# A ring of seven instead of eight buffers for expert rows, and four more rows of the output projection's weights kept on the chip

## The chip, the cores and the metric

One NeuronCore of a Trainium2 chip runs the whole step. Five engines work side by side: PE (matrix products), DVE (vector work), ACT (activations and scaled copies), POOL (here mostly the issuing of gathers) and SP (here only the issuing of transfers). The core's 16 DMA engines move data between HBM and the on-chip memory (SBUF). The metric is the device time in microseconds of one execution of the program; lower is better.

## What is computed

One layer of a hybrid decoder for 512 prompt tokens (behind 16 learned tokens) and 64 sample tokens. All data are float32. Cut to what matters here:

```python
xn = rmsnorm(hp, norm1[l])
qa, ka, va, qkv_b, z, b_raw, a_raw = project(xn, w_in[l], q_norm[l], k_norm[l])
...
hp = hp + merge_heads(oa, ob, z, lam_init, attn_subln[l], gdn_norm[l], w_out[l], hp.dtype)
hp = hp + peer_ffn(rmsnorm(hp, norm2[l]), peer_wq[l], peer_keys[l], peer_u[l], peer_v[l])
```

`merge_heads` ends in `y @ w_out`, the output projection (a 1024 x 1024 matrix). `peer_ffn` is the expert layer: every token picks 128 of 16384 experts (8 heads, 16 each); an expert is a row `u` and a row `v` of 1024 numbers:

```python
h = jnp.einsum('td,thkd->thk', xb, u[e]).astype(jnp.float32)
w = (gate * jax.nn.gelu(h, approximate=False)).astype(xb.dtype)
return jnp.einsum('thk,thkd->td', w, v[e])
```

## The kernel before

**Tokens.** They are worked on in four blocks of 128 prompt tokens and a last one with the 64 sample tokens (two experts of a sample token share a slot). A first phase, to some 480 us, projects all tokens, does the short convolution, the paged attention of the sample tokens and the first part of the delta network. In a second phase the experts of block t are worked off, and the attention, the output projection and the choice of experts of block t + 1 are done between them.

**A slot.** The second phase has 576 slots (128 for each prompt block, 64 for the last). For slot m POOL gathers one expert for each of 128 tokens: 128 rows of 2048 numbers (`u` and `v` side by side), 1 MB, into buffer m % RING of the tile `uv` (line 971). DVE multiplies `u` with the tokens and sums (line 1786), ACT makes the slot's weight (lines 1348, 1352) and puts it on a diagonal (line 1359), and PE adds weight times `v` to the block's sum by two products with that diagonal (line 2217). For 111 of the slots DVE adds `v` itself (line 1759). Only then is the buffer free. POOL issues gather m once the buffer of slot m - RING is free; it waits for that in front of every gather:

```python
if m >= RING and added_here(m - RING):
    pool.wait_ge(s_va, added_before(m - RING) + 1)
elif m >= RING:
    pool.wait_ge(s_vd, m - RING + 1 - added_before(m - RING))
```

**Order.** Every engine's order is fixed when the program is written: each piece of work is a generator that yields a due time, and `advance` emits the piece with the earliest one. In the second phase due times count slots; POOL emits what is due by `m - RING + USED` ahead of gather m, the other engines what is due by m.

**The output projection.** Its weights come in two halves of 512 output columns; a half has eight rows (128 x 512 numbers, 256 KB each). A block's products run in `mix` (line 2126; for the sample tokens line 2145) and take row k of a half by `mixer_row` (line 547). Rows 0 to 5 of the first half and rows 0 and 1 of the second stay in the tile `mix_kept` from the first block on (`KEPT = (6, 2)`, loaded by line 777). The other rows, two of the first half and six of the second, are loaded again for each block into `zone` (line 778), in which the expert layer's route weights follow (line 780, four loads of 2.25 MB a block). SP issues all of these, in `route_loads`.

**Room.** The last part of SBUF is used twice. In the first phase it holds the tokens turned round, the input weights, and other tiles, of which `taps`, the weights of the short convolution, lies near the end; in the second phase `uv` lies there.

Of the kernel before, what the change touches and what calls it, by code (L numbers as in the profile page):

```python
# [8 lines left out]
F32 = mybir.dt.float32  # L9
# [7 lines left out]
D = 1024  # L17
# [10 lines left out]
HW = NH * HD  # L28
CONV_W = 4
# [3 lines left out]
NT = PT + 1  # L33
# [38 lines left out]
PIECES = 6  # L72
PAGE_BUFFERS = 8
NPAIR = DB // 2
RING = 8
DIAGS = 4
WEIGH, SUM, USED = 0.4, 1.3, 1.5
NORMED = (9.2, 9.4)
# [2 lines left out]
ZONE = KC * HW + 4 * NK  # L81
FRONT = 11680
NEVER = 1.0e9
KEPT = (6, 2)
DMA_RING = 2048


# [88 lines left out]
def advance(streams, until):  # L176

    while min(s.due for s in streams) <= until:
        s = min(streams, key=lambda s: s.due)
        s.due = next(s.steps, NEVER)  # L180
# [55 lines left out]
def route_at(n, k):  # L236
    return SLOTS * (n - 1) + (74 + 1.05 * k if n < PT else 36 + 1.05 * k + (14 if k >= 4.9 else 0))
# [8 lines left out]
def hybrid_step(nc: bass.Bass, i, o, stay_table, early_table, past_table):  # L246

    ctx = ExitStack()
    with ctx:
        def keep(name, shape, dt=F32):  # L250
            return ctx.enter_context(nc.sbuf_tensor("sb_" + name, shape, dt))

        def stage(names):

            out = {}
            with ExitStack() as s:
                for name, (shape, dt) in names.items():
                    out[name] = s.enter_context(nc.sbuf_tensor("sb_" + name, shape, dt))
            return out

        def sem(name):
            return nc.alloc_semaphore(name)

        stay = keep("stay", [128, NSTAY])
        mix_kept = keep("mix_kept", [128, sum(KEPT), HW])
        minus_half = keep("minus_half", [128, 16])
        sizes = (HW, 2 * HW, 3 * HW, HW, NH * TOK, NT * HW, HW, NH * NSAMP, NH * 128)
        held = keep("held", [128, sum(sizes)])
# [21 lines left out]
        def st(name, rows=128, width=None):  # L290
# [19 lines left out]
        G = stage({  # L310
            "xn2": ([128, 2, D], F32), "q2T": ([128, 2, 4, 128], F32), "gain2T": ([128, KC], F32),
            "score": ([128, 4, 4, NK], F32),
            "Sw": ([128, 4 * NPOS + 2 * SEQ], F32), "wTm": ([META, 2, 128], F32),
            "nm": ([128, 2, 2], F32), "Z": ([128, 2, 2], F32), "rz": ([128, 2, 2], F32),
            "ass": ([128, NH], F32), "ams": ([128, NH], F32), "ars": ([128, NH], F32),
            "ss2": ([128, NT], F32), "ms2": ([128, NT], F32), "rstd2": ([128, NT], F32),
            "eidx": ([128, 2, SLOTS], U32), "best": ([128, 2 * TOPK], F32), "gate": ([128, 2, SLOTS], F32),
            "gmax": ([128, 2, TOPK], F32), "gsum": ([128, 2], F32),
# [6 lines left out]
        F.update(stage({  # L325
            "xnT": ([128, KC * TOK], F32), "w": ([128, PIECES, KC // 4, HW], F32), "wba": ([128, KC, 2 * NH], F32), "raw": ([128, 2, HW], F32), "qkn": ([128, 2, HW], F32),
            "qst": ([128, 2, HW], F32), "gains": ([128, 2 * DQ + HD], F32),
            "taps": ([128, CONV_W, HW], F32), "rstd": ([128, NT], F32), "ss8": ([128, 2, 8], F32), "ms8": ([128, 2, 8], F32), "rstd8": ([128, 2, 8], F32),
        }))
        G.update(stage({"uv": ([128, RING, 2 * D], F32)}))  # L330
        G["S"] = G["Sw"][:, 0:4 * NPOS].rearrange("p (a n) -> p a n", a=2)
        G["wT"] = G["Sw"][:, 4 * NPOS:].rearrange("p (a n) -> p a n", a=2)
        samp_x = G["Sw"][:, 2 * NPOS:2 * NPOS + D]
# [66 lines left out]
        s_conv = sem("conv_steps")  # L400
# [133 lines left out]
        xn2, score, eidx, best, gate, uv = (G[name] for name in ("xn2", "score", "eidx", "best", "gate", "uv"))  # L534

        def route_part(n, part):

            if n >= PT - 1 and part in (2, 3):
                first = edges[1] + ZONE * (part - 2)
                return held[:, first:first + ZONE]  # L540
            return R["zone"][:, part % 2, :]

        def weights_part(n, part):

            return route_part(n, part)[:, 0:KC * HW].rearrange("p (k n) -> p k n", k=KC)

        def mixer_row(n, half, k):

            return mix_kept[:, KEPT[0] * half + k, :] if k < KEPT[half] else weights_part(n, half)[:, k, :]

        def keys_part(n, part):

# [40 lines left out]
        s_wr = [sem(f"route_weights_loaded{r}") for r in range(2)]  # L593
        s_xs = sem("sample_tokens_loaded_again")
        s_kept = [sem(f"kept_mixer_weights_loaded{half}") for half in range(2)]
        s_g2 = sem("gain2_loaded")
        s_x2 = sem("x_loaded_again")
        s_mxp = sem("mix_transposed")
# [11 lines left out]
        s_gtd = sem("places_found_and_gate_steps")  # L610
        s_uv = [sem(f"expert_rows{j}") for j in range(RING)]
        s_h = sem("activations")
# [19 lines left out]
        def pick_of(t, n):  # L632

            return picks_before(t) + [n // TOPK in heads for heads in picks(t)].index(True)
# [6 lines left out]
        def added_here(m):  # L641
            t, n = ALL[m]
            return t < PT and n % 5 in (1, 4) and (t + 1 == PT or 33 <= n < 50 or 72 <= n < 105)

        def added_before(m):
            return sum(added_here(k) for k in range(m))
# [4 lines left out]
        with nc.Block() as block:  # L651

            @block.sync
            def _(sp):
# [96 lines left out]
                def route_loads(n):  # L751
                    apart = n + 1 == PT
                    for part in range(6):
                        yield route_at(n, (-18, -17, -1, 2, 8, 11)[part] if apart else (-18, -17, 4, 7, 24, 32)[part])
                        if part < 2:
                            sp.wait_ge(s_ob, 2 * (n + 2))
                            if apart:
                                sp.wait_ge(s_sTc, 2 * NH + 1)
                        elif apart and part < 4:
                            sp.wait_ge(s_pv, NH * PT)  # L760
                            sp.wait_ge(s_vst, 16 * (NT + 1))
                            sp.wait_ge(s_vec, 3 * NT)
                            sp.wait_ge(s_DT, 2 * NT)
                            sp.wait_ge(s_tr, 4 * NT)
                            sp.wait_ge(s_wr[part % 2], 16 * (3 * n + 1))
                        elif apart:
                            sp.wait_ge(s_yp, 2 * (PT + 1))
                            sp.wait_ge(s_wr[part % 2], 16 * (3 * n + 2))
                        elif part < 4:
                            sp.wait_ge(s_yp, 2 * n + part - 1)  # L770
                        else:
                            sp.wait_ge(s_s2p, 4 * n + part - 3)
                        if part < 2:
                            first = KEPT[part]
                            weights = i["w_mixer"][part].rearrange("p (k n) -> p k n", k=KC)
                            if n == 0:
                                sp.dma_start(mix_kept[:, KEPT[0] * part:KEPT[0] * part + first, :], weights[:, 0:first, :]).then_inc(s_kept[part], 16)
                            sp.dma_start(weights_part(n, part)[:, first:, :], weights[:, first:, :]).then_inc(s_wr[part % 2], 16)
                        else:
                            sp.dma_start(route_part(n, part), i["w_route"][part - 2]).then_inc(s_wr[part % 2], 16)  # L780
# [69 lines left out]
            def _(pool):  # L850
# [109 lines left out]
                for m, (t, n) in enumerate(ALL):  # L960
                    advance(work, m - RING + USED)
                    if m == 0:
                        for s_last, total in second_done:
                            pool.wait_ge(s_last, total)
                    if first_slot(t, n):
                        pool.wait_ge(s_idx, pick_of(t, n) + 1)
# [4 lines that stand above are left out]
# [820 lines left out]
            def _(pe):  # L1791
# [315 lines left out]
                def mix(n):  # L2107
                    yield route_at(n, 0)
                    pe.wait_ge(s_oa, 2 * (n + 2))
                    pe.wait_ge(s_ob, 2 * (n + 2))  # L2110
                    if n:
                        pe.wait_ge(s_s2c, 4 * n)
                    for half in range(2):
                        for k in range(4):
                            ins = nc.tensor.transpose(bank[4 + half][:, k * 128:(k + 1) * 128], hres[:, n % 2, (4 * half + k) * 128:(4 * half + k + 1) * 128], st("ident"))
                        ins.then_inc(s_mxp, 1)
                    for half in range(2):
                        for part in range(2):
                            yield route_at(n, 2 + 3 * half + 1.5 * part)
                            if part == 0:  # L2120
                                pe.wait_ge(s_wr[half], 16 * (3 * n + 1))
                                pe.wait_ge(s_mxc, 2 * (n + 1))
                                if n == 0:
                                    pe.wait_ge(s_kept[half], 16)
                            for k in range(4 * part, 4 * part + 4):
                                ins = nc.tensor.matmul(bank[6 + half][:, :], lhsT=R["rT"][:, k, :], rhs=mixer_row(n, half, k), start=k == 0, stop=k == KC - 1)  # L2126
                        ins.then_inc(s_yp, 1)
# [141 lines left out]
```

## Time and profile before

| what | value |
|---|---|
| time, median of 3 runs | 2041.9 us (2041.38 to 2045.73) |
| the profiled execution's own time | 2044.21 us |
| its span, first to last instruction | 2042.4 us |
| PE / DVE / ACT / POOL busy | 83% / 65% / 39% / 38% of the span |
| moved by DMA | 759.68 MB, of it 622.22 MB on POOL's queue |
| POOL idle ahead of a gather until PE freed a buffer (line 2217) | 657.7 us, 382 times |
| DVE idle until a gather had landed | 270.7 us, 204 times |
| a gather, from issue to landing | 13.9 us median |

The profile is of one execution. Its time exceeds its span by 1.8 us, which lie around the first and last instruction. Idle time of an engine is put down to what ended it. The share of DMA is the mean busy share of the 16 DMA engines; it can come out a little over 1. The time from issue to landing of a transfer holds its own movement and the time in which it stood behind others.

### The profile page before, as it was taken

How to read it: one execution, taken by the hardware profiler on the slowest of the kernel's cores; microseconds unless marked ns; L12 is line 12 of the kernel's file. 1: busy time of each engine (PE TensorE's matmuls, PEld its weight loads, DVE VectorE, ACT ScalarE, POOL GpSimd, SP SyncE). 2: the span in 40 equal slices, each digit the busy share in tenths (PEclk: the TensorE clock that was granted, in tenths of full speed). 3: DMA queues.
4: the chain of work that ended last, by engine and by line, in shares of the span. 5: the costliest groups of instructions: out<-in, count | busy, mean ns of one | idle time of the engine just before them, and what ended most of it. 6: DMA issues, size and time to landing. Idle time of an engine off the chain costs nothing.

```text
span 2042.4 us, 20301 instructions
## 1 busy us (share of the span) xinstructions
PE 1701.8 (83%) x6211; PEld 854.2 (42%) x6211; DVE 1335.3 (65%) x3023; ACT 800.8 (39%) x2371; POOL 774.7 (38%) x670
## 2 busy tenths in 40 slices
PE   6898899988998978889897889978897657866777
PEld 2333465547553445445344435543463214522111
DVE  1345514336897567887755888874588977679544
ACT  1344312123546433463633446363244423333432
POOL 2211100111444443536344343533444455554442
PEclk9899999999998998999998999998999788987999
DMA  9999623148999999999999999999999999999997
GB/s 344 365 373 368 226 68 114 47 148 322 415 406 420 427 428 427 427 423 414 426 399 427 427 426 403 422 413 384 408 426 426 418 427 427 426 427 426 428 426 323
DMA packets 137157, 759.68 MB, mean 372 GB/s; under 512 B 15279, under 2 KB 24255, under 8 KB 60616
## 3 DMA queue, kind: packets, MB, share of 16 engines
q0 software_dynamic: 88448, 622.22, 73.4%
q1 hardware_dynamic: 44112, 124.93, 16.5%
q10 hardware_dynamic: 4488, 11.23, 1.4%
q8 instruction: 49, 0.80, 0.1%
q14 instruction: 60, 0.49, 0.1%
HBM read 742.35 MB, written 16.26 MB: 371 GB/s over the span
## 4 chain that ended last, share of the span: by engine, by line
PE 36%; DMA 29%; DVE 18%; ACT 8%; issue 4%; POOL 2%; ACTq 0%; DVEq 0%; POOLq 0%
DMA sb_uv<-in_peer_uv,sb_eidx 25%; PE bank L2217 17%; DVE sb_uv L1786 7%; PE bank L1807 6%; DMA sb_hres<-pre_conv 2%; PE bank L2184 2%; PE bank L2126 2%; DVE sb_hres L1759 2%; POOL sb_uv L971 1%; ACT sb_diag L1359 1%; ACT L1348 1%; ACT sb_ew L1352 1%; DMA sb_zone<-in_w_route 1%; PE bank L1921 1%; PE bank L1933 1%
## 5 line engine op out<-in xcount | busy, mean ns | idle before, releaser
L2217 PE MATMUL bank<-sb_uv,sb_diag 128*128 128x512 f32 (+1 forms) x1860 | 956.1, 651 | 273.4 <-ACT sb_diag L1359 263.3
L971 POOL DMA_INDIRECT sb_uv<-in_peer_uv,sb_eidx x576 | 692.2, 1202 | 850.0 <-PE bank L2217 657.7
L1786 DVE CUSTOM_DVE_ANT_0 sb_uv<-sb_uv,sb_xn 128x1024 f32<-128x1024 f32 x576 | 698.3, 1220 | 272.7 <-DMA sb_uv<-in_peer_uv,sb_eidx 270.7
L2217 PEld LDWEIGHTS bank<-sb_uv,sb_diag 128*128 128x128 f32 (+1 forms) x1860 | 336.6, 196 | 773.4 <-ACT sb_diag L1359 445.5
L1348 ACT ACTIVATE sb_gel<-sb_h 128x1 f32<-128x1 f32 x576 | 116.3, 202 | 753.3 <-DVE sb_h L1786 750.3
L1807 PE MATMUL bank<-sb_w,sb_xnT 128*128 128x512 f32 (+1 forms) x560 | 265.2, 615 | 18.3 <-DVE sb_xnT L1377 8.4
L1359 ACT ACTIVATE sb_diag<-sb_stay,sb_ew 128x128 f32<-128x128 f32 (+1 forms) x465 | 183.2, 394 | 47.0 <-PE bank L2217 2.8
L1352 ACT ACTIVATE sb_ew<-sb_gel,sb_gate 128x1 f32<-128x1 f32 x576 | 169.7, 295 | 20.1 <-ACT sb_gel L1348 0.4
L1807 PEld LDWEIGHTS bank<-sb_w,sb_xnT 128*128 128x128 f32 (+1 forms) x560 | 98.2, 186 | 140.5 <-issue 118.7
L1759 DVE SCALAR_TENSOR_TENSOR sb_hres<-sb_uv,sb_ew,sb_hres 128x1024 f32<-128x1024 f32 x111 | 142.1, 1280 | 0.1
L2184 PEld LDWEIGHTS bank<-sb_rT,sb_zone 128*128 128x128 f32 x1024 | 122.9, 194 | 20.8 <-issue 20.3
L2184 PE MATMUL bank<-sb_rT,sb_zone 128*128 128x128 f32 x1024 | 124.3, 277 | 2.1 <-issue 1.8
L895 POOL TENSOR_TENSOR sb_rstd<-sb_ms,sb_minus_half 128x8 f32<-128x8 f32 (+1 forms) x10 | 16.4, 1640 | 112.4 <-DVE sb_ms L1463 112.4
L1786 DVE DVE_READ_ACCUMULATOR2_ANT sb_h<- 128x1 f32 x576 | 46.8, 81 | 0.0
L1348 ACT ACT_TABLE_LOAD x33 | 42.3, 1283 | 0.6
L1435 DVE TENSOR_TENSOR sb_xin<-sb_xin,sb_taps 128x2048 f32<-128x2048 f32 (+1 forms) x8 | 18.3, 2289 | 32.5 <-DMA sb_xin<-pre_conv 32.5
L1690 DVE FIND_INDEX8 sb_tix<-sb_top,sb_score 128x8 uint32<-128x128 f32 x144 | 38.4, 283 | 0.0
L1686 DVE MAX8 sb_top<-sb_score 128x8 f32<-128x128 f32 x144 | 31.4, 278 | 7.0 <-ACT sb_score L1320 6.9
L1527 DVE TENSOR_TENSOR sb_X<-sb_X,bank 128x256 f32<-128x256 f32 (+1 forms) x36 | 14.7, 407 | 30.5 <-PE bank L1933 28.9
L2184 PEld LDWEIGHTS bank<-sb_rT,sb_held 128*128 128x128 f32 x256 | 30.9, 192 | 6.2 <-issue 6.2
L2126 PE MATMUL bank<-sb_mix_kept,sb_rT 128*128 128x512 f32 x64 | 32.2, 641 | 1.3 <-issue 0.8
L2184 PE MATMUL bank<-sb_rT,sb_held 128*128 128x128 f32 x256 | 31.2, 275 | 0.0
(352 smaller groups left out, 1581.5 us busy)
## 6 DMA issues: line engine op xcount, KB each, us to landing
sb_zone<-in_w_route SPq DMA_DIRECT2D x14, 2304.0 KB, 11.8
sb_w<-in_w_sections SPq DMA_DIRECT2D x40, 512.0 KB, 9.0
sb_uv<-in_peer_uv,sb_eidx POOLq DMA_INDIRECT x576, 13.9
sb_sS<-in_cache_kT SPq DMA_DIRECT2D x32, 256.0 KB, 8.7
sb_zone<-in_cache_kT SPq DMA_DIRECT2D x32, 256.0 KB, 7.2
sb_held<-in_cache_v SPq DMA_DIRECT2D x32, 256.0 KB, 7.6
sb_zone<-in_cache_v SPq DMA_DIRECT2D x32, 256.0 KB, 9.0
sb_hres<-pre_conv POOLq DMA_DIRECT2D x6, 1024.0 KB, 7.9
```

The lines of the kernel that those rows point to most:

```text
L971: nc.gpsimd.indirect_dma_start(uv[:, m % RING, :], None, i["peer_uv"], bass.IndirectOffsetOnAxis(ap=eidx[:, t % 2, n:n + 1], axis=0)).then ...
L1348: nc.scalar.activation(G["gel"][:, at], G["h"][:, at], ACT.Gelu).then_inc(s_dg, 1)
L1352: nc.scalar.activation(G["ew"][:, at], G["gel"][:, at], ACT.Copy, scale=gate[:, t % 2, n:n + 1]).then_inc(s_dg, 1)
L1359: nc.scalar.activation(G["diag"][:, d % DIAGS, 0:cols], eye, ACT.Copy, scale=G["ew"][:, at]).then_inc(s_dg, 1)
L1686: n_top = count.inc(nc.vector.max(top[:, q, k:k + 8], sets[q]), s_tk)
L1690: n_used = count.inc(nc.vector.max_index(tix[:, q, k:k + 8], top[:, q, k:k + 8], sets[q]), s_cut if k and q == quads[-1] else s_tk)
L1759: nc.vector.scalar_tensor_tensor(hres[:, t % 2, :], uv[:, m % RING, D:2 * D], G["ew"][:, m % 8:m % 8 + 1], hres[:, t % 2, :], ALU.mult, AL ...
L1786: nc.vector.tensor_tensor_reduce(out=uv[:, m % RING, 0:D], in0=uv[:, m % RING, 0:D], in1=xn2[:, t % 2, :], scale=1.0, scalar=0.0, op0=ALU. ...
L1807: ins = nc.tensor.matmul(bank[b][0:rows, :], lhsT=xT(t)[:, kk, :], rhs=F["w"][:, piece % PIECES, kk % 2, :], start=kk == 0, stop=kk == KC - 1)
L2126: ins = nc.tensor.matmul(bank[6 + half][:, :], lhsT=R["rT"][:, k, :], rhs=mixer_row(n, half, k), start=k == 0, stop=k == KC - 1)
L2184: ins = nc.tensor.matmul(bank[6 + j % 2][:, 128 * s:128 * s + 128], lhsT=weights_part(n, g + 2)[:, k, 128 * s:128 * s + 128], rhs=R["rT"][ ...
L2217: ins = nc.tensor.matmul(bank[half][0:rows, :], lhsT=G["diag"][:, d % DIAGS, 0:rows], rhs=uv[:, m % RING, D + 512 * half:D + 512 * half + ...
```

## The change

`RING` goes from 8 to 7, so `uv` gives back 8 KB in each partition. They become the tile `mix_more`: rows 2 to 5 of the second half of the output projection's weights (`KEPT` is now (6, 6)). The first eight kept rows stay where they were, in `mix_kept`. `taps` moves to the end of the first phase's tiles, so that `mix_more` lies over it and over nothing else that is still in use. For the first block SP waits until the convolution's steps are done, loads the four rows into `mix_more`, then the two into `mix_kept`, then the remaining two into `zone`. For the three later blocks the second half's load into `zone` falls from six rows to two. PE waits for the new load ahead of both halves of the first block's products.

```diff
-RING = 8
+RING = 7
...
-KEPT = (6, 2)
+KEPT = (6, 6)
+FIRST_KEPT = 8
...
-        mix_kept = keep("mix_kept", [128, sum(KEPT), HW])
+        mix_kept = keep("mix_kept", [128, FIRST_KEPT, HW])
...
-        G.update(stage({"uv": ([128, RING, 2 * D], F32)}))
+        G.update(stage({"uv": ([128, RING, 2 * D], F32), "mix_more": ([128, sum(KEPT) - FIRST_KEPT, HW], F32)}))
...
-            return mix_kept[:, KEPT[0] * half + k, :] if k < KEPT[half] else weights_part(n, half)[:, k, :]
+            row = KEPT[0] * half + k
+            if k >= KEPT[half]:
+                return weights_part(n, half)[:, k, :]
+            return mix_kept[:, row, :] if row < FIRST_KEPT else G["mix_more"][:, row - FIRST_KEPT, :]
...
                             if n == 0:
-                                sp.dma_start(mix_kept[:, KEPT[0] * part:KEPT[0] * part + first, :], weights[:, 0:first, :]).then_inc(s_kept[part], 16)
+                                here = min(first, FIRST_KEPT - KEPT[0] * part)
+                                if here < first:
+                                    sp.wait_ge(s_conv, 9 * NT)
+                                    sp.dma_start(G["mix_more"][:, :, :], weights[:, here:first, :]).then_inc(s_more, 16)
+                                sp.dma_start(mix_kept[:, KEPT[0] * part:KEPT[0] * part + here, :], weights[:, 0:here, :]).then_inc(s_kept[part], 16)
                             sp.dma_start(weights_part(n, part)[:, first:, :], weights[:, first:, :]).then_inc(s_wr[part % 2], 16)
...
                                     pe.wait_ge(s_kept[half], 16)
+                                    pe.wait_ge(s_more, 16)
```

SP's order at the first block's weights, before and then with the change (a kept row is 512 numbers wide, so 128x2048 is four rows):

```order
316 L777 DMA sb_mix_kept<-in_w_mixer 128x3072
317 L778 DMA sb_zone<-in_w_mixer 128x1024
318 L777 DMA sb_mix_kept<-in_w_mixer 128x1024
319 L778 DMA sb_zone<-in_w_mixer 128x3072
320 L715 DMA q_spilled<-sb_qst 128x512 x2
```

```order
316 L786 DMA sb_mix_kept<-in_w_mixer 128x3072
317 L787 DMA sb_zone<-in_w_mixer 128x1024
318 L785 DMA sb_mix_more<-in_w_mixer 128x2048
319 L786 DMA sb_mix_kept<-in_w_mixer 128x1024
320 L787 DMA sb_zone<-in_w_mixer 128x1024
```

Four rows go from the load into `zone` to one of their own, ahead of the other two of that half; SP issues five transfers here in place of four, of the same sum.

SP's order at the second block's weights (the third and fourth read alike), before and with the change:

```order
326 L728 DMA sb_held<-kqv_spilled 128x1536
327 L734 DMA sb_held<-z_spilled 128x512
328 L778 DMA sb_zone<-in_w_mixer 128x1024
329 L778 DMA sb_zone<-in_w_mixer 128x3072
330 L749 DMA sb_held<-q_spilled 128x512
```

```order
327 L733 DMA sb_held<-kqv_spilled 128x1536
328 L739 DMA sb_held<-z_spilled 128x512
329 L787 DMA sb_zone<-in_w_mixer 128x1024 x2
330 L754 DMA sb_held<-q_spilled 128x512
331 L794 DMA sb_Sw<-in_x_prompt 128x1024
```

The transfer of six rows is now one of two; nothing else moved.

POOL's order in the second phase, from its beginning, before and with the change (line 971, now 980, is the gather):

```order
66 L971 DMA sb_uv<-in_peer_uv,sb_eidx 128x2048 x51
67 L901 TENSOR_TENSOR sb_ors<-sb_oms,sb_minus_half 128x4
68 L971 DMA sb_uv<-in_peer_uv,sb_eidx 128x2048 x25
69 L945 TENSOR_TENSOR sb_ars<-sb_ams,sb_minus_half 128x4
70 L971 DMA sb_uv<-in_peer_uv,sb_eidx 128x2048 x16
```

```order
66 L980 DMA sb_uv<-in_peer_uv,sb_eidx 128x2048 x50
67 L910 TENSOR_TENSOR sb_ors<-sb_oms,sb_minus_half 128x4
68 L980 DMA sb_uv<-in_peer_uv,sb_eidx 128x2048 x25
69 L954 TENSOR_TENSOR sb_ars<-sb_ams,sb_minus_half 128x4
70 L980 DMA sb_uv<-in_peer_uv,sb_eidx 128x2048 x16
```

Each of POOL's small operations stands one gather earlier, and so behind the same freed buffer as before.

## Rows read from the trace of the kernel before

**Rows 1.** The page, GB/s moved in each of 40 slices of 51.06 us.
```profile
GB/s 344 365 373 368 226 68 114 47 148 322 415 406 420 427 428 427 427 423 414 426 399 427 427 426 403 422 413 384 408 426 426 418 427 427 426 427 426 428 426 323
```

**Rows 2.** Waits, whole span: engine, tile, line, what ended it; us, times, longest.
```profile
POOL sb_uv L971 <- PE bank L2217: 657.7, 382, 14.6
```

**Rows 3.** Stretches: window, its us, busy us of engines, PEclk, DMA share, GB/s.
```profile
1640.00:1840.00 200.00, 143.81 (x498) 74.72 (x499) 144.56 (x234) 67.63 (x229) 108.96 (x82) 0.90 1.01 427
```

**Rows 4.** DMA issues, whole span: transfer, queue, count, KB each, median us to landing.
```profile
sb_zone<-in_w_mixer SPq DMA_DIRECT2D x4, 1536.0 KB, 13.3
```

**Rows 5.** DMA issues, 1640 to 1840 us: count, median us to landing.
```profile
sb_uv<-in_peer_uv,sb_eidx POOLq DMA_INDIRECT x81, 14.5
```

**Rows 6.** DMA and its issues, 520 to 605 us.
```profile
DMA packets 5114, 36.21 MB, mean 426 GB/s; under 512 B 569, under 2 KB 569, under 8 KB 825
...
sb_uv<-in_peer_uv,sb_eidx POOLq DMA_INDIRECT x31, 10.0
```

**Rows 7.** Lines 777 and 778 on SP: ns of one issue, first and last start.
```profile
L777 SPq DMA_DIRECT2D sb_mix_kept<-in_w_mixer x2: 333/378/423, 414.1 to 415.0; - x2
...
L778 SPq DMA_DIRECT2D sb_zone<-in_w_mixer x8: 332/426/532, 414.5 to 1329.3; - x8
```

**Rows 8.** Line 2126: ns of one (least, median, most), first and last start.
```profile
L2126 PE MATMUL bank<-sb_mix_kept,sb_rT x64: 592/592/1191, 444.1 to 1426.8; 128*128 128x512 f32 x64
```

**Rows 9.** Timeline of POOL, five places: start, us, line, operation, idle before.
```profile
507.28 0.94 POOL L971 DMA_INDIRECT sb_uv<-in_peer_uv,sb_eidx  x1 [14.60 <-PE bank L2217]
510.04 0.94 POOL L971 DMA_INDIRECT sb_uv<-in_peer_uv,sb_eidx  x1 [1.82 <-PE bank L2217]
...
606.51 1.75 POOL L971 DMA_INDIRECT sb_uv<-in_peer_uv,sb_eidx  x1 [5.24 <-PE bank L2217]
...
608.57 0.94 POOL L971 DMA_INDIRECT sb_uv<-in_peer_uv,sb_eidx  x1 [0.30 <-issue]
...
1024.47 1.92 POOL L971 DMA_INDIRECT sb_uv<-in_peer_uv,sb_eidx  x1 [6.14 <-PE bank L2217]
1026.70 0.94 POOL L971 DMA_INDIRECT sb_uv<-in_peer_uv,sb_eidx  x1 [0.31 <-PE bank L2217]
...
1378.24 1.28 POOL L971 DMA_INDIRECT sb_uv<-in_peer_uv,sb_eidx  x1 [6.07 <-PE bank L2217]
1381.01 0.95 POOL L971 DMA_INDIRECT sb_uv<-in_peer_uv,sb_eidx  x1 [1.48 <-PE bank L2217]
...
1447.38 1.91 POOL L971 DMA_INDIRECT sb_uv<-in_peer_uv,sb_eidx  x1 [5.09 <-PE bank L2217]
...
1450.24 1.45 POOL L971 DMA_INDIRECT sb_uv<-in_peer_uv,sb_eidx  x1 [0.18 <-issue]
```

**Rows 10.** Stretches around those places, and two stretches without a stop.
```profile
605.00:610.00 5.00, 5.00 (x23) 2.62 (x21) 4.90 (x9) 0.98 (x4) 2.88 (x3) 1.00 0.70 238
910.00:940.00 30.00, 30.00 (x131) 18.29 (x130) 20.27 (x41) 12.81 (x44) 15.27 (x13) 1.00 1.00 403
1025.00:1030.00 5.00, 5.00 (x16) 2.37 (x15) 0.59 (x2) 2.68 (x10) 3.27 (x3) 1.00 0.72 221
1375.00:1380.00 5.00, 5.00 (x12) 2.46 (x12) 4.86 (x10) 2.27 (x9) 1.28 (x1) 0.66 0.54 229
...
1600.00:1625.00 25.00, 17.05 (x28) 6.26 (x26) 24.35 (x53) 12.23 (x35) 13.55 (x11) 0.78 1.00 407
```

**Rows 11.** Waits of DVE, 620 to 640 us.
```profile
DVE sb_uv L1786 <- DMA sb_uv<-in_peer_uv,sb_eidx: 2.5, 2, 1.5
```

**Rows 12.** Waits of DVE, 966 to 990 us.
```profile
DVE sb_uv L1786 <- DMA sb_uv<-in_peer_uv,sb_eidx: 5.0, 3, 2.4
```

**Rows 13.** Waits of DVE, 1328 to 1350 us.
```profile
DVE sb_uv L1786 <- DMA sb_uv<-in_peer_uv,sb_eidx: 3.2, 2, 2.0
```

**Rows 14.** Timeline of DVE, 1018 to 1040 us: start, us, line, operation, idle before.
```profile
1032.08 0.17 DVE L1611 TENSOR_SCALAR sb_ams<-sb_ass 128x4 f32<-128x4 f32 x1 [6.49 <-ACT sb_xn L1226]
```

**Rows 15.** Line 971: from issue to landing, all 576 gathers.
```profile
DMA to landing us min/median/max: 5.6/13.9/25.5
```

## What the change will do to the time

> **What bounds the kernel now.** I read first the strip of GB/s by slices [rows 1]: from the tenth slice on, which is the second phase, it stands at 426 to 428 in most slices and falls to 384 to 415 in some. So the second phase is bound by moved bytes most of the time, and something stops the transfers in places. A stretch without such places shows the ceiling: 427 GB/s for 200 us at a DMA share of 1.01 [rows 3]. One gather is 128 x 2048 x 4 bytes = 1,048,576 bytes; at 427 GB/s that is 2.46 us, the unit of all that follows.
>
> Then the waits: POOL, which issues the gathers, stands idle 657.7 us until PE frees a buffer [rows 2]. That number looks like a ring that is too small, and is not: a queue that is full makes POOL wait just as well. What tells the two apart is how many gathers are on their way. In the clean stretch a gather lands 14.5 us after its issue [rows 5], which at 2.46 us each is 5.9 gathers under way; between 520 and 605 us it is 10.0 us, or 4.1 gathers, and the rate is still 426 GB/s [rows 6]. So where the transfers are the bound, one gather less under way (4.9) costs nothing: the time in the queue gets 2.46 us shorter instead.
>
> Last, the places where the transfers stop. I looked on POOL's timeline for long waits that are followed by a burst of issues, and found five: at 507, 606, 1024, 1378 and 1447 us POOL was idle 14.60, 5.24, 6.14, 6.07 and 5.09 us and then issued gather upon gather [rows 9]. PE had been held up, all landed rows lay unused and nothing was left to transfer: around the second, third and fourth the rate falls to 238, 221 and 229 GB/s over 5 us [rows 10]. There the ring is the bound, and there the eighth buffer counts.
>
> **The change, part by part.** *Bytes.* A block's second half of the projection's weights is now loaded as 1536 KB [rows 4]; two rows are 512 KB, so each of the three later blocks moves 1024 KB less, exactly one gather: 2.46 us each, 7.4 us in all. Is that time on the path? The last of the three loads is issued at 1329.3 us [rows 7], and in the 20 us around and behind it DVE waits 3.2 us for expert rows; behind the two others, from 620 and from 966 us on, it waits 2.5 and 5.0 us [rows 11 to 13], each time at least 2.46 us. I take the full **-7.4 us**; the bounds are that and nothing (if DVE then waits for something else). In the first block the sum of bytes is the same.
>
> *First block.* SP issues the four loads from 414.1 us on, the third of them at 415.0 us, and a load of six rows lands 13.3 us after its issue at the median [rows 4, 7]; PE takes them from 444.1 us on [rows 8]. One issue more, half a microsecond, and PE's wait for the new load lie in some 15 us of slack. SP's wait for the convolution adds none, since SP already waits for the convolution's outputs ahead of all these loads. If that cover were gone, it would cost the issue, 0.5 us. I take 0. Nothing queued behind on SP in that stretch is nearer to its use.
>
> *PE and POOL.* The products of the projection read another tile, with as many instructions and shapes. POOL's small operations follow the same freed buffer as before. 0 for both.
>
> *The ring.* With seven buffers, every gather that waits for a buffer is issued when the next one comes free. In a burst the delay is the distance between its first two issues, at most the 2.46 us that the transfer itself takes: with the five places in order 2.76, 2.06, 2.23, 2.77 and 2.86 us [rows 9], so 2.46 + 2.06 + 2.23 + 2.46 + 2.46 = 11.7 us. Each is lost for good if the transfers are the bound from there to the next place. The bounds are 0 (DVE has other work, below) and 12.3 us (five times 2.46); I take 11.7, since these rows are of the very places. Two more stretches run without a stop but below the ceiling: 403 GB/s for 30 us and 407 for 25 us [rows 10], with gathers as few as in the stretch of 10.0 us or fewer. Against 427 that is 30 x (1 - 403/427) = 1.7 and 25 x (1 - 407/427) = 1.2 us lost now. One gather less under way takes at least nothing; I let the loss double, **2.9 us**, and keep 0 and 2 x 2.46 = 4.9 us as bounds. The ring's price is 11.7 + 2.9 = **14.6 us**.
>
> Beside this the Trainium skill, "Perfetto Trace Analysis", section "Optimization Strategy", says that the same gap recurring on the engine that ought to be saturated can mean too little room for the next tile, the number of buffers among it. By that rule the five stops are a shortage of buffers, and the change takes from what is short; the rows agree as to where, and the sum above is only dearer by it if more stops appear than the five.
>
> **Sum.** 14.6 - 7.4 = +7.2 us. On the profiled execution's own 2044.2 us (span 2042.4 and 1.8 around it) that is 2051.4; that execution lies 2.3 us above the median, so on 2041.9 us I forecast **2049.1 us**. By the bounds: the dearest here is 12.3 + 4.9 - 7.4 = +9.8 us, and without the saving +17.2. About 0.2%, 4 us, is what a measurement of this kernel can tell from no change.
>
> **Rivals.**
>
> *The stops are absorbed in part.* Right after the stop at 1024 us DVE is not short of rows: at 1032 us it had waited 6.49 us for ACT's squares, which wait for PE [rows 14]. A gather that lands 2.3 us later inside such a wait delays nobody. The stops at 1378 and 1447 us belong to the same work of the next block. If those three cost nothing, the ring's price is 2.46 + 2.06 + 2.9 = 7.4 us, as much as the saving: 2041.9 us. For it: the wait is longer than the delay. Against it: the transfers had stopped and have to make up for it afterwards at a ceiling that they already reach. Chance 0.23.
>
> *Faster: seven buffers are enough.* If a gather or two under way filled the engines and PE's burst refilled the queue faster than it drains, no stop would get longer, and only the bytes would count: 2041.9 - 7.4 = 2034.5 us. It decides at the five places: if the 5 us windows there keep their 221 to 238 GB/s, this is it. For it: the stops begin when PE is held up, which no buffer changes. Against it: a lone gather needs 5.6 us to land [rows 15], over two transfer times, so a queue of one or two does not fill the engines. Chance 0.15. The Trainium skill, "DMA: Bandwidth & Descriptors", section "Anatomy of one DMA — SWDGE (gpsimd) path", gives 2.0 us plus the bytes over 436 GB/s for one transfer, 4.4 us for a gather by my estimate; by that two under way would keep the engines full, and the eighth buffer would be free to give. This trace's least, 5.6 us, speaks for three or more.
>
> *The saved bytes are not seen.* If the three loads end in a time in which DVE turns to other waits, the ring's price stands alone: 2041.9 + 14.6 = 2056.5 us. DVE's waits behind them barely cover it in the first case (2.5 us). Chance 0.09.
>
> *Too few under way over long stretches.* Where a gather lands after 10.0 us now, three instead of four would be under way. If the rate there fell from 426 to the 403 GB/s of the worst such stretch, each gather would take 2.60 us instead of 2.46. That concerns the 85 us of [rows 6] and the two stretches named above, 140 us together: 140 x (427/403 - 1) = 8.3 us in place of the 2.9, so +12.6 us, 2054.5 us; more of the second phase is alike, so it can pass 2060. Against it: rows that have landed and wait for DVE would give way first, before the number under way does. Chance 0.06.
>
> **How the numbers follow.** The forecast has 0.47, the rivals 0.23, 0.15, 0.09 and 0.06. The forecast's own range is 2045 to 2054 us; 0.03 of its chance lies below 2046 us. Faster by over 0.2%: 0.15. Within 0.2%: 0.23 + 0.03 = 0.26. Slower: 0.44 + 0.09 + 0.06 = 0.59. The range of 8 in 10 reaches down into the absorbed case and past it, to 2037 us, and up to 2058 us; it leaves out most of the faster rival and the upper end of the last one.
>
> **What will show it.** Right: in the clean stretch a gather lands after about 14.5 - 2.46 = 12.0 us at an unchanged 427 GB/s; at the five places the rate over 5 us falls further or the stop lasts some 2 us longer; the bytes moved fall by 3.1 MB; DVE's wait for expert rows grows there and shrinks behind the three loads; the first gather is issued as early as before, since the first phase is untouched. Wrong: the distance from before does not grow in steps of about 2 us at these places, or it grows evenly over the long stretches (the last rival), or the clean stretch falls below 427 GB/s with five under way, which would break the whole reckoning.

## The result and the profile after

The changed kernel takes 2051.33 us (median of 14 runs, 2047.80 to 2059.99), the kernel before beside it 2043.35 us (median of 14). The ratio is 1.0043 with a 95% interval of 1.003 to 1.0056: **8.8 us slower, between 6.1 and 11.4**. Forecast were 7.2 us, and 2037 to 2058 us as the range.

The profiled execution of the changed kernel took 2048.26 us with a span of 2046.5 us, 4.1 us over the one shown of before. Of these, 2.6 us arise ahead of the first gather (485.5 us in place of 482.9). Runs whose first phase is that of the kernel before issue it between 481.0 and 490.5 us, so that part need not be an effect of the change.

From the page after: the strip of GB/s by slices, to be held against [rows 1], and the moved bytes (before, 759.68 MB in all; POOL's queue moves 622.22 MB in both):

```profile
GB/s 342 351 376 376 222 73 113 47 132 312 411 400 417 422 427 426 427 415 420 421 405 426 427 427 392 420 382 400 407 426 408 423 428 427 427 427 427 427 426 328
DMA packets 137301, 756.53 MB, mean 370 GB/s; under 512 B 15295, under 2 KB 24271, under 8 KB 61144
```

3.15 MB less are moved, as the edit says, and yet the strip is lower in most slices from the eleventh to the thirty-first (in a few, the twenty-first and the twenty-eighth among them, it is higher). Waits after, to be held against [rows 2] and against DVE's 270.7 us, 204 times:

```profile
POOL sb_uv L980 <- PE bank L2227: 681.5, 393, 15.7
...
DVE sb_uv L1795 <- DMA sb_uv<-in_peer_uv,sb_eidx: 295.3, 223, 6.7
```

DVE waits 24.6 us more for expert rows. From 1640 us on, where the transfers are the bound, nothing is lost, and the queue is one transfer time shorter, as forecast (answers to [rows 3, 5]; the first row is the stretch, the second the issues in it):

```profile
1640.00:1840.00 200.00, 142.82 (x500) 74.04 (x500) 143.74 (x224) 67.44 (x229) 109.38 (x83) 0.92 1.01 427
```

```profile
sb_uv<-in_peer_uv,sb_eidx POOLq DMA_INDIRECT x82, 12.1
```

In the stretch of [rows 6], from 520 to 605 us, it is otherwise:

```profile
DMA packets 4974, 35.16 MB, mean 414 GB/s; under 512 B 557, under 2 KB 557, under 8 KB 813
...
sb_uv<-in_peer_uv,sb_eidx POOLq DMA_INDIRECT x33, 9.4
```

426 GB/s have become 414. A gather lands only 0.6 us sooner than before, not 2.46. I read this as a queue that was no longer than the transfers needed, so that one gather less leaves the engines short.

**A measure for all runs.** What the second phase loses to idle DMA engines is the time of a stretch less its bytes over 427 GB/s. I call it the shortage. From 510 to 1640 us, before and after:

```profile
DMA packets 64261, 472.17 MB, mean 418 GB/s; under 512 B 7101, under 2 KB 7613, under 8 KB 9789
```

```profile
DMA packets 64152, 468.27 MB, mean 414 GB/s; under 512 B 7085, under 2 KB 7597, under 8 KB 10157
```

Before it is 1130 - 472,170/427 = 24.2 us, after 33.3 us: 9.1 us more, against 7.4 us less to move. So much of it lies around the five stops, in five windows (their us, PE, PEld, DVE, ACT, POOL, PEclk, DMA share, GB/s), before and then after:

```profile
505.00:520.00 15.00, 15.00 (x32) 6.48 (x31) 10.81 (x41) 6.53 (x23) 7.10 (x7) 0.89 0.96 364
600.00:620.00 20.00, 18.11 (x73) 8.94 (x72) 17.79 (x38) 9.45 (x29) 9.11 (x7) 0.93 0.93 374
1020.00:1040.00 20.00, 17.33 (x44) 7.99 (x44) 9.69 (x18) 8.11 (x35) 10.24 (x9) 0.91 0.90 354
1370.00:1390.00 20.00, 17.46 (x55) 9.19 (x54) 8.76 (x19) 12.09 (x40) 6.83 (x7) 0.91 0.88 344
1440.00:1460.00 20.00, 20.00 (x66) 10.33 (x65) 10.64 (x16) 8.18 (x28) 8.32 (x7) 1.00 0.96 385
```

```profile
505.00:520.00 15.00, 13.25 (x27) 5.81 (x28) 10.98 (x45) 7.45 (x27) 6.31 (x6) 0.89 0.85 318
600.00:620.00 20.00, 16.83 (x72) 8.52 (x72) 19.63 (x47) 9.10 (x28) 8.48 (x8) 1.00 0.97 387
1020.00:1040.00 20.00, 17.41 (x44) 8.13 (x44) 9.90 (x18) 9.18 (x35) 8.84 (x9) 0.91 0.91 361
1370.00:1390.00 20.00, 17.46 (x55) 9.05 (x54) 9.07 (x19) 12.31 (x40) 6.49 (x8) 0.91 0.84 317
1440.00:1460.00 20.00, 20.00 (x65) 10.22 (x65) 10.74 (x18) 8.19 (x28) 9.07 (x7) 1.00 0.94 379
```

Each window's us times (1 - GB/s/427) gives 2.2, 2.5, 3.4, 3.9 and 2.0 = 14.0 us before and 3.8, 1.9, 3.1, 5.2 and 2.2 = 16.2 us after. Only the first and the fourth stop are deeper by more than 1 us. **Of the 9.1 us more, 6.9 lie outside the stops.** That is not what the forecast said.

One execution is thin ground, so other runs' profiles have to bear it out. Run 1 below has seven buffers and all else as before; its shortage from 510 to 1640 us is 1130 - 469,260/427 = 31.0 us, and its windows are these:

```profile
DMA packets 63861, 469.26 MB, mean 415 GB/s; under 512 B 7057, under 2 KB 7569, under 8 KB 9745
...
600.00:620.00 20.00, 16.44 (x72) 8.31 (x71) 18.70 (x43) 9.86 (x30) 9.05 (x7) 1.00 0.96 373
1020.00:1040.00 20.00, 17.56 (x55) 8.71 (x53) 9.58 (x20) 11.95 (x40) 8.92 (x10) 1.00 0.96 379
1370.00:1390.00 20.00, 16.40 (x59) 8.77 (x58) 12.47 (x23) 12.76 (x42) 7.79 (x7) 1.00 0.89 350
1440.00:1460.00 20.00, 20.00 (x54) 9.24 (x53) 13.49 (x21) 9.08 (x31) 10.13 (x8) 1.00 0.94 382
505.00:520.00 15.00, 15.00 (x33) 6.54 (x32) 9.23 (x32) 4.90 (x18) 7.58 (x8) 0.91 0.83 304
```

Runs 3 and 7 are the kernel before up to slot 415, which is to some 1630 us. The table has the shortage in the five windows and in the eleven stretches into which they and the marks 705, 840, 900, 1200, 1240 and 1560 us cut the time from 520 to 1640 us:

| profile | buffers there | five stops, us | between them, us |
|---|---|---|---|
| before | eight | 14.0 | 11.3 |
| run 3 | eight | 10.7 | 12.5 |
| run 7 | eight | 13.6 | 12.6 |
| changed kernel | seven | 16.2 | 17.8 |
| run 1 | seven | 14.8 | 19.2 |

Between the stops both profiles with seven lie 5 us and more above all three with eight. At the stops the three with eight differ among themselves by as much as seven add. A single stretch proves little: from 520 to 600 us run 3 moved 417 GB/s with eight buffers, the changed kernel 413. From 510 us on, the shortage of the three with eight is 24.5, 22.0 and 26.2 us by the same windows. So differences of up to 4 us between two profiles mean nothing, and the times below, each from 5 to 12 runs against 22 or 23 of the kernel before, carry the verdicts.

### The profile page after: what moved, and what is told of

Its sections match the earlier page's. It is cut to its first block, busy times and chain, and to the rows that moved or that the text cites. A ratio compares the mean times of both kernels' runs of the same rounds, so it can differ in the third digit from the quotient of the medians.

```text
span 2046.5 us, 20305 instructions
## 1 busy us (share of the span) xinstructions
PE 1700.0 (83%) x6211; PEld 853.8 (42%) x6211; DVE 1336.2 (65%) x3023; ACT 802.0 (39%) x2371; POOL 766.2 (37%) x670
## 3 DMA queue, kind: packets, MB, share of 16 engines
q0 software_dynamic: 88448, 622.22, 73.6%
## 4 chain that ended last, share of the span: by engine, by line
PE 38%; DMA 29%; DVE 18%; ACT 8%; issue 4%; POOL 2%; SPq 1%; ACTq 0%; DVEq 0%; POOLq 0%
DMA sb_uv<-in_peer_uv,sb_eidx 23%; PE bank L2227 18%; DVE sb_uv L1795 8%; PE bank L1816 7%; PE bank L2194 3%; PE bank L2136 2%; DMA sb_hres<-pre_conv 2%; DVE sb_hres L1768 2%; POOL sb_uv L980 1%; ACT sb_diag L1368 1%; DMA sb_w<-in_w_sections 1%; ACT L1357 1%; ACT sb_ew L1361 1%; DMA sb_zone<-in_w_route 1%; PE bank L1930 1%
## 5 line engine op out<-in xcount | busy, mean ns | idle before, releaser
L980 POOL DMA_INDIRECT sb_uv<-in_peer_uv,sb_eidx x576 | 683.4, 1187 | 863.2 <-PE bank L2227 681.5
L1361 ACT ACTIVATE sb_ew<-sb_gel,sb_gate 128x1 f32<-128x1 f32 x576 | 169.7, 295 | 20.1 <-ACT sb_gel L1357 0.4
L1357 ACT ACT_TABLE_LOAD x33 | 42.3, 1283 | 0.6
L1536 DVE TENSOR_TENSOR sb_X<-sb_X,bank 128x256 f32<-128x256 f32 (+1 forms) x36 | 14.7, 407 | 28.7 <-PE bank L1942 27.3
L1444 DVE TENSOR_TENSOR sb_hres<-sb_hres,sb_taps 128x2048 f32<-128x2048 f32 (+1 forms) x7 | 16.0, 2291 | 25.6 <-DMA sb_hres<-pre_conv 25.6
## 6 DMA issues: line engine op xcount, KB each, us to landing
sb_uv<-in_peer_uv,sb_eidx POOLq DMA_INDIRECT x576, 11.2
```

What stands on the lines that cost most here:

```text
L980: nc.gpsimd.indirect_dma_start(uv[:, m % RING, :], None, i["peer_uv"], bass.IndirectOffsetOnAxis(ap=eidx[:, t % 2, n:n + 1], axis=0)).then ...
L1357: nc.scalar.activation(G["gel"][:, at], G["h"][:, at], ACT.Gelu).then_inc(s_dg, 1)
L1361: nc.scalar.activation(G["ew"][:, at], G["gel"][:, at], ACT.Copy, scale=gate[:, t % 2, n:n + 1]).then_inc(s_dg, 1)
L1444: count.done(nc.vector.tensor_tensor(x, x, cw[0:rows], ALU.mult), s_conv)
```

## The experiments

In runs 3 to 7 and 9 to 11 the eight buffers stay and POOL is only held back: it waits for the buffer of `depth` slots earlier, so that at most `depth` are in use.

```diff
+                freed = 0
                 for m, (t, n) in enumerate(ALL):
-                    advance(work, m - RING + USED)
+                    depth = 7 if m >= 416 else RING
+                    advance(work, m - depth + USED)
...
+                    while freed <= m - depth:
+                        if added_here(freed):
+                            pool.wait_ge(s_va, added_before(freed) + 1)
+                        else:
+                            pool.wait_ge(s_vd, freed + 1 - added_before(freed))
+                        freed += 1
```

Differences are ratio times median of the kernel before beside it, with 95% intervals:

| run | what | us against before |
|---|---|---|
| 1 | seven buffers, all else as before | +12.9 (9.4 to 16.6) |
| 2 | eight buffers, 3.1 MB less | -4.9 (-7.8 to -2.0) |
| 3 | seven from slot 416 on | +1.6 (-1.2 to +4.3) |
| 4 | seven up to slot 415 | +17.2 (13.3 to 21.1) |
| 5 | seven around the five stops | +11.6 (7.4 to 15.7) |
| 6 | seven up to 415, but not there | +9.0 (4.3 to 13.7) |
| 7 | five from slot 416 on | +37.6 (32.9 to 42.3) |
| 8 | nine buffers, four kept rows | -1.0 (-4.3 to +2.0) |
| 9 | seven where transfers are the bound | +1.2 (-1.6 to +4.1) |
| 10 | seven in the rest between the stops | +7.3 (4.7 to 10.0) |
| 11 | six up to slot 415 | +56.8 (52.1 to 61.5) |
| 12 | nine buffers, bytes as before | -8.4 (-11.6 to -5.1) |

**Run 1, the ring alone** (`RING = 7` and nothing else).

> Ring of seven, nothing else changed: the same eight kept rows, the same bytes as before. If the stops set the ring's price (the forecast): +14.6 us on the kernel before, of it about 2 us at each of five places. If the stops are absorbed in part: +7.4 us. If seven buffers are enough: 0. The changed kernel measured +8 us; so whatever this shows beyond +8 us is what the saved bytes give back, 7.4 us if they are all seen.

+12.9 us: near the forecast's 14.6, and above the 7.4 at which the stops would be absorbed in part (the interval begins at 9.4). Seven buffers are not free.

**Run 2, the bytes alone.**

```diff
+            if n and half and KEPT[half] <= k < KEPT[0]:
+                return mix_kept[:, k, :]
...
+                            first = KEPT[0] if n else first
```

> Ring of eight, and in the three later blocks the second half of the projection's weights is loaded as two rows in place of six; left out are the four rows themselves (the products take rows of the first half in their place, same instructions and shapes). If the saved bytes are seen in full: -7.4 us. If DVE then waits for something else: near 0.

-4.9 us; 7.4 lies inside the interval, 0 does not. Runs 1 and 2 together give 12.9 - 4.9 = +8.0 us, the changed kernel measured +8.8: the two parts of the change add up, and no third is needed. The intervals are wide enough to hide one of a few microseconds.

**Runs 3 and 4, where the ring counts** (`depth` as above, and `7 if m < 416 else RING`).

> Eight buffers, but from slot 416 on POOL waits for the buffer of seven slots earlier, so that at most seven are in use, as with a ring of seven. The forecast: 0 us, since the transfers are the bound there and 4.9 gathers under way instead of 5.9 fill the engines; a gather lands after about 12 us in place of 14.5, at 427 GB/s. If fewer gathers under way cost something over long stretches: over +2 us.

> Eight buffers, but up to slot 415 POOL waits for the buffer of seven slots earlier; from there on eight again. The forecast: the whole price of the ring of seven, as in the run with seven buffers alone (+14.6 us, or whatever that one shows), since all five stops and both slower stretches lie here. If the price were spread over the whole second phase, about seven tenths of it.

+1.6 us with 0 inside, and +17.2 us. As far as can be measured, the whole price arises up to slot 415. Run 4 should equal run 1; its +17.2 and the other's +12.9 have overlapping intervals, and I read them as one price of 13 to 17 us. In run 4's profiled execution 7.6 of the 23.5 us over the span of before lie ahead of the first gather (490.5 us in place of 482.9), where the edit does nothing; how much of this is in its other executions is not known. In run 3 the clean stretch is nearly as forecast: a gather lands after 12.0 us, at 425 GB/s.

**Runs 5 and 6, stops or stretches** (`depth` 7 inside, then outside, of the four ranges of slots named).

> Eight buffers, but around the five stops alone (slots 0 to 17, 40 to 55, 192 to 207, 320 to 356; 87 of 576 slots) POOL waits for the buffer of seven slots earlier. If the stops set the price: nearly all that the ring of seven alone cost (+11.7 us by the forecast, 9 to 13 by what was measured). If the price is spread over long stretches: 87/416 of it, about +3 us.

> The complement: seven up to slot 415 except around the five stops, where it is eight. If the stops set the price: +2.9 us or less. If it is spread: +10 us.

+11.6 us from 87 slots, the forecast's 11.7; but +9.0 us between them, where 2.9 or less was expected. Both theories are half right. A buffer around a stop is worth most by far (11.6 us in 87 slots, 9.0 in 329), yet the long stretches are not free. The profiles agree: run 5's loses 19.2 us in the five windows and 15.5 between them, run 6's 6.1 and 27.7.

**Runs 9 and 10, which stretches.**

> Eight buffers, seven in three stretches between the stops where DVE waits for expert rows most of the time and route weights are loaded beside the gathers (slots 80 to 127, 208 to 255, 357 to 379; 119 slots). If a queue that is long anyway gives a gather away for nothing, as from slot 416 on: 0. If the 9 us that the run between the stops cost are spread evenly over its 329 slots: +3.3 us.

> Eight buffers, seven in the other 210 slots between the stops (18 to 39, 56 to 79, 128 to 191, 256 to 319, 380 to 415), where rows lie landed and DVE is late for them, four gathers are under way, and the rate is full or just below. If the backlog gives way first: near 0, and the 9 us between the stops stay unexplained. If the ring runs short here in small: all of the 9 us. If spread evenly: +5.7 us.

+1.2 us with 0 inside, and +7.3 us. Where route weights are loaded beside the gathers, giving one away costs nothing that can be measured. Most of the price between the stops, and perhaps all, comes from the stretches in which DVE is late. Run 10's profile shows what happens at the stops when only the stretches ahead are held back, in the same windows:

```profile
505.00:520.00 15.00, 15.00 (x32) 6.40 (x31) 10.63 (x41) 6.39 (x22) 7.63 (x8) 0.89 0.96 362
600.00:620.00 20.00, 16.44 (x72) 8.51 (x72) 18.70 (x42) 9.86 (x30) 9.05 (x7) 1.00 1.01 428
1020.00:1040.00 20.00, 17.56 (x54) 8.99 (x55) 9.58 (x21) 12.65 (x42) 9.81 (x9) 1.00 1.01 409
1370.00:1390.00 20.00, 16.40 (x52) 8.25 (x51) 11.21 (x21) 12.14 (x38) 7.08 (x7) 0.91 1.00 404
1440.00:1460.00 20.00, 20.00 (x64) 10.07 (x63) 11.67 (x18) 8.68 (x30) 8.66 (x8) 1.00 1.01 425
```

and its stretch from 520 to 605 us and whole from 510 to 1640 us:

```profile
DMA packets 4873, 34.45 MB, mean 405 GB/s; under 512 B 543, under 2 KB 543, under 8 KB 799
```

```profile
DMA packets 64083, 470.86 MB, mean 417 GB/s; under 512 B 7084, under 2 KB 7596, under 8 KB 9772
```

The stops are all but gone: 2.3, 0, 0.8, 1.1 and 0.1 = 4.3 us in place of 14.0. The stretches have taken their place, 405 GB/s instead of 426 in the one shown; in all the shortage is 1130 - 470,860/427 = 27.3 us, and between the stops, by the eleven stretches, it is 23.5 us against 11.3 before. **In this run part of the shortage only changes its place**, and run 6, held back in the same way, shows it too.

It does not follow that the same happens in the changed kernel. Where the depth goes from seven back to eight, the edit itself hands POOL a free buffer: slot 40, the first of the second stop's range, was issued with nothing to wait for, and the three behind it alike:

```profile
591.10 1.97 POOL L975 DMA_INDIRECT sb_uv<-in_peer_uv,sb_eidx  x1 [0.30 <-issue]
```

So a buffer withheld in the stretch is spent just ahead of the stop, and PE's hold-up meets a queue that has been filled afresh. That cannot be all of it: the fifth stop, at slot 347, lies 27 slots behind the last such border and is gone too. With seven everywhere nothing is handed back, and the stops are no shallower than before (16.2 and 14.8 us); there the shortage between the stops comes on top. The parts (11.6 + 7.3 + 1.2 = 20.1) come to more than the whole (13 to 17), as they would if a gather held back in one place were missed less in the next. But the intervals are wide, and the changes of depth at each border may have a price of their own; why the parts do not add up is not shown.

**Runs 8 and 12, a ninth buffer** (`RING = 9`, `KEPT = (2, 2)`; one semaphore with a wait for 32 serves both kept loads, and `h`, `gel`, `ew` have nine columns). Run 12 also has

```diff
+            if n and half == 0 and 2 <= k < 6:
+                return mix_kept[:, k - 2, :]
...
+                            first = 6 if n and part == 0 else first
```

> The trade the other way round: nine buffers, and four kept rows in place of eight (two of each half), so 3.1 MB more are moved; the small tiles with one number a slot get nine columns, and one semaphore serves both loads of kept rows. The bytes cost +4.9 us (as the run with fewer bytes showed) to +7.4 us. If a ninth buffer shortens the five stops as the eighth did, by 11 to 15 us: -4 to -10 us in all, faster than both kernels. If what is left of the stops bounds it (the five windows lack some 9 us of transfer): -1 to -4 us. If a ninth buffer is no use: +5 to +7 us.

> Nine buffers and four kept rows, but in the three later blocks as few rows are loaded as in the kernel before; left out are four rows of the first half (the products take kept rows in their place). This is the ninth buffer alone. If it shortens the stops as the eighth did: -11 to -15 us. If the bytes cost 4.9 us in the run with nine buffers and all of them: -6 us.

-1.0 us with 0 inside, and -8.4 us. The ninth buffer is worth 8.4 us, less than the eighth. With its bytes it is level with the kernel before. The difference of the two runs, 7.4 us, is what the same 3.1 MB cost by the forecast's arithmetic. In run 12 the stops are gone and the shortage from 510 to 1640 us is 1130 - 478,570/427 = 9.2 us, 15.0 less than before; the time shows 8.4 of them (5.1 to 11.6), and where the rest goes is open:

```profile
505.00:520.00 15.00, 15.00 (x33) 6.51 (x32) 12.48 (x46) 6.65 (x23) 8.28 (x8) 0.91 1.01 427
600.00:620.00 20.00, 14.60 (x54) 6.71 (x52) 18.83 (x36) 8.56 (x30) 10.18 (x8) 1.00 1.01 422
...
1370.00:1390.00 20.00, 17.14 (x43) 7.84 (x42) 7.92 (x14) 6.98 (x28) 9.80 (x9) 0.91 1.01 427
```

```profile
DMA packets 65147, 478.57 MB, mean 424 GB/s; under 512 B 7206, under 2 KB 7718, under 8 KB 9894
```

**Run 11, six.**

> Eight buffers, but up to slot 415 POOL waits for the buffer of six slots earlier. If every buffer costs the same at the same five places: twice the price of seven, +26 to +34 us. If with six the stretches with four gathers under way run short as well: more, +40 us or over.

+56.8 us, three to four times the price of seven, as expected (+40 us or over) if the stretches run short as well. Each buffer less costs more than the one before: -8.4 for nine, 0 for eight, +12.9 to +17.2 for seven, +56.8 for six.

**Run 7, how few fill the engines.**

> Eight buffers, but from slot 416 on POOL waits for the buffer of five slots earlier. A buffer is held some 5 us after its rows have landed, so five leave 5 x 2.46 - 5 = 7.3 us for issue and landing, 3 gathers under way. If three do not fill the engines, as the slower stretches of the kernel before say (403 to 407 GB/s): 160 slots at 2.55 to 2.60 us, +14 to +22 us. If two transfers under way fill them: within 2 us.

+37.6 us, 1.7 times the most that was expected. Its stretch from 1660 to 1860 us, and the issues in it:

```profile
1660.00:1860.00 200.00, 137.92 (x476) 72.39 (x476) 123.52 (x177) 59.73 (x201) 90.67 (x72) 0.87 0.97 373
```

```profile
sb_uv<-in_peer_uv,sb_eidx POOLq DMA_INDIRECT x71, 8.7
```

## Why the prediction was right, and where it was not

**The bytes: right.** Forecast -7.4 us; -4.9 (-7.8 to -2.0) alone, and 7.4 between the two runs with nine buffers. Behind the three loads DVE waits 2.1, 3.7 and 3.2 us for expert rows, where it waited 2.5, 5.0 and 3.2; that these waits shrink by a transfer each is not what the profile shows, so the saving is seen in the times alone.

**The first block, PE, POOL at nothing: right as far as shown.** SP issues the loads from 416.75 to 418.65 us, and the slowest of the loads of kept rows lands 11.2 us after its issue; the first product starts at 446.7 us (before 444.1, [rows 8]), with the loads as far ahead of it as before.

**No price where the transfers are the bound: right.** +1.6 and +1.2 us with 0 inside both intervals; 12.1 us to landing and 427 GB/s, forecast 12.0 and 427.

**The five stops, 11.7 us: the size right, the place not.** Held back around the stops alone, the kernel loses 11.6 us. But with seven everywhere the stops in the profiles deepen by 2.2 us in sum (0.8 in run 1), not 11.7, and the growth lies between them (6.5 and 7.9 us), which by the forecast's own signs speaks against it. The step that failed is "each is lost for good if the transfers are the bound from there to the next place": it priced every stop by its own two issues, as if the stretch ahead brought it the same number of landed rows. It does not; the stretch ahead runs short itself.

**The two slower stretches, 2.9 us: mis-sized, and mostly in the wrong place.** In the changed kernel's profile the two windows named lose no more than before, 1.8 + 0.5 = 2.3 us against 2.9 (in run 1, at 397 and 393 GB/s, 4.1):

```profile
910.00:940.00 30.00, 30.00 (x130) 18.25 (x129) 22.01 (x45) 15.10 (x48) 14.43 (x12) 1.00 0.99 401
...
1600.00:1625.00 25.00, 16.93 (x27) 6.14 (x26) 24.31 (x57) 11.34 (x31) 13.14 (x11) 0.77 1.01 419
```

That is at most 1.2 of the 6.5 and 7.9 us. The 210 slots of run 10, among them those of the two windows, cost 7.3 us. The forecast put the other stretches at nothing, and the fault is in "between 520 and 605 us it is 10.0 us, or 4.1 gathers, and the rate is still 426": that shows that four are enough, not that three are. With one less, that stretch fell to 414 GB/s here, to 405 in run 10. The last rival had this term at 8.3 us and so was near in the price; it put it on top of stops that deepen in full (2054.5 us), which they do not.

**The sum: right, in part by luck.** 14.6 for the ring against 12.9 measured (17.2 by the other way), 7.4 for the bytes against 4.9: +7.2 against +8.8, each within its interval. Inside the ring's price two errors cancel: the stretches between the stops cost more than the forecast gave them, and stops and stretches together less than the sum of both. Added up as the forecast adds, the measured parts would give 20.1 - 4.9 = 15.2 us.

**The rivals.** Partly absorbed stops would have made the ring cost 7.4 us; run 1 excludes that. A free ring is excluded by the same run. Nor do two gathers under way fill the engines, since in run 7 three move 373 GB/s. By the cost of one transfer in the Trainium skill, "DMA: Bandwidth & Descriptors", section "Anatomy of one DMA — SWDGE (gpsimd) path", as the forecast used it, two would; the measurement decides against reading it that way. Unseen bytes are excluded by run 2.

**No version beats the kernel before.** Runs 2 and 12 are faster but leave rows out; with all rows the trade of run 12 is run 8, level. So a buffer for four rows costs 8.8 us in one direction and brings nothing that can be measured in the other.

## What to carry to other kernels

Before a ring is made shorter, ask of each stretch how many transfers are under way and at which number its rate starts to fall; only where the queue is longer than that is a buffer free. Price the stretches ahead of a stop together with the stop, since a buffer withheld in one can shorten the other (run 10), and do not add the prices of the parts. The long wait of the issuing engine for a free buffer tells neither way: it was 657.7 us before and 681.5 after, and the ring's price was 13 to 17.

## What was not expected of the hardware

In run 7, with three gathers under way, each took 8.7 us from issue to landing, not the 7.3 us reckoned before the run, and the engines moved 373 GB/s at a DMA share of 0.97, where 427 GB/s go with 1.01: an eighth fewer bytes, and hardly a change in the share. Here the busy share of DMA hardly shows a queue that is too short; the GB/s do.

And the price of a buffer is far from even: 8.4 us for the ninth, 13 to 17 for the eighth, some 40 for the seventh.
